# Filling three waits of TensorE with identity-times-ones matmuls in a two-block transformer kernel

## What is computed

```
first_block:  proj = rmsnorm(x) @ w_in ; two attentions (indexed sparse, latent)
              merged = sigmoid(g_a)*(o_a @ w_branch_a) + sigmoid(g_b)*(o_b @ w_branch_b)
              h = x + merged @ w_out
              h = h + (silu(gate)*val) @ w_down,   gate, val = conv(rmsnorm(h) @ w_up)
              x = rmsnorm(h)
second_block: h = [16 meta tokens; x] ; h = h + 0.5*swiglu(rms_norm(h))
              xn = rms_norm(h, norm_mix)
              merged = sum over 3 mixers of sigmoid(xn @ w_gate) * (y @ w_branch)
              h = h + merged @ w_out ; h = h + 0.5*swiglu(rms_norm(h))
              return rms_norm(h, final_norm)[:, 16:]
```

## Time and profile before

| | |
|---|---|
| median of 3 runs | 2298.59 us (2298.19 to 2300.34) |
| the profiled execution's own time | 2298.83 us |
| its span, first to last instruction | 2297.0 us |
| mean granted TensorE clock | 0.987 |
| TensorE matmul busy | 2209.4 us, 96% |
| DVE busy | 1257.7 us, 55% |
| ACT busy | 901.5 us, 39% |
| POOL busy | 220.3 us, 10% |

### The profile page before, as it was taken

The page is one execution under the profiler, slowest core; times in us unless marked ns, Lnnn a source line. Parts: engine busy times, 40 slices in busy tenths (PEclk is TensorE's granted clock), DMA queues, the critical chain, the costliest instruction groups (busy, mean ns, idle before and its releaser), DMA issues.

```text
span 2297.0 us, 35675 instructions
## 1 busy us (share of the span) xinstructions
PE 2209.4 (96%) x12408; PEld 1805.9 (79%) x12408; DVE 1257.7 (55%) x2672; ACT 901.5 (39%) x1803; POOL 220.3 (10%) x201
## 2 busy tenths in 40 slices
PE   6999999999999999999999799999999999999998
PEld 4557766777888889999999677777777777888887
DVE  5878877457745755542443545554545655443442
ACT  4465445444423444321232344443444433322333
POOL 0100033420000012000001000111100121000001
PEclk8999999999999999999999999999999999999999
DMA  3111211234443342333333222344333333333332
GB/s 104 38 38 39 65 42 51 60 106 139 145 135 88 94 151 76 89 117 101 91 90 101 73 80 80 79 102 105 94 84 100 84 92 92 91 104 89 91 108 74
DMA packets 400391, 205.64 MB, mean 90 GB/s; under 512 B 68956, under 2 KB 393928, under 8 KB 400284
## 3 DMA queue, kind: packets, MB, share of 16 engines
q1 hardware_dynamic: 399365, 203.83, 31.1%
q10 hardware_dynamic: 919, 0.43, 0.1%
HBM read 201.94 MB, written 14.80 MB: 94 GB/s over the span
## 4 chain that ended last, share of the span: by engine, by line
PE 82%; DVE 4%; ACT 2%; issue 2%; POOL 0%; DVEq 0%; ACTq 0%; POOLq 0%
PE acc L1159 52%; PE acc L1445 15%; PE acc L1205 5%; PE sco L1480 2%; PE acc L1544 1%; PE sco L1247 1%; PE acc L1540 1%; DVE w_lo L2219 1%; PE acc L1294 1%; PE sco L1520 1%; PE acc L1520 0%; PE sco L1500 0%; PE acc L1281 0%; PE sco L1271 0%; PE acc L1271 0%
## 5 line engine op out<-in xcount | busy, mean ns | idle before, releaser
L1672 ACT ACTIVATE w_hi<-raw 128x512 fp32r<-128x512 f32 (+4 forms) x656 | 371.9, 614 | 697.6 <-PE acc L1159 663.7
L2219 DVE TENSOR_TENSOR w_lo<-raw,w_hi 128x512 fp32r<-128x512 f32 (+4 forms) x656 | 425.1, 688 | 142.6 <-ACT w_hi L1672 138.3
L1159 PE MATMUL acc<-xn_hi,w_hi 128*128 128x512 f32 (+1 forms) x1408 | 421.0, 340 | 2.1 <-DVE qbuf L2769 2.1
L1159 PE MATMUL acc<-xn_lo,w_hi 128*128 128x512 f32 (+1 forms) x1408 | 422.0, 340 | 0.0
L1159 PE MATMUL acc<-xn_hi,w_lo 128*128 128x512 f32 (+1 forms) x1408 | 420.3, 339 | 0.0
L1159 PEld LDWEIGHTS acc<-xn_hi,w_hi 128*128 128x128 f32 x1408 | 241.9, 188 | 35.8 <-DVE qbuf L2769 3.0
L1159 PE MATMUL acc<-hid_hi,w_hi 128*128 128x512 f32 (+1 forms) x832 | 261.4, 349 | 7.0 <-DVE hid_lo L2711 7.0
L1159 PEld LDWEIGHTS acc<-xn_lo,w_hi 128*128 128x128 f32 x1408 | 241.2, 188 | 31.1 <-issue 0.5
L1159 PEld LDWEIGHTS acc<-xn_hi,w_lo 128*128 128x128 f32 x1408 | 241.5, 188 | 30.0
L1159 PE MATMUL acc<-hid_lo,w_hi 128*128 128x512 f32 (+1 forms) x832 | 263.0, 351 | 0.0
L1159 PE MATMUL acc<-hid_hi,w_lo 128*128 128x512 f32 (+1 forms) x832 | 262.2, 349 | 0.0
(11 more groups left out here) (393 smaller groups left out, 3040.7 us busy)
## 6 DMA issues: line engine op xcount, KB each, us to landing
raw<-in_w_ffn_in SPq DMA_DIRECT2D x176, 256.0 KB, 3.0
raw<-in_w_in SPq DMA_DIRECT2D x118, 256.0 KB, 3.1
raw<-in_w_up SPq DMA_DIRECT2D x88, 256.0 KB, 3.0
raw<-in_w_ffn_out SPq DMA_DIRECT2D x32, 384.0 KB, 3.4
raw<-in_w_gate SPq DMA_DIRECT2D x48, 256.0 KB, 3.2
raw<-in_w_ffn_out SPq DMA_DIRECT2D x32, 320.0 KB, 3.8
raw<-in_w_out SPq DMA_DIRECT2D x32, 256.0 KB, 3.1
bias<-grids_dram SPq DMA_DIRECT2D x64, 128.0 KB, 3.0
```

The source lines that it names most:

```text
L1159: mm = pe.matmul(acc[0:m, 2 * slot + b, 0:size], w[slot][:, t, 0:m], x[:, place(t), c:c + size], start=(t == 0 and w is w_hi and x is xh), ...
L1672: act.activation(w_hi[slot][:, a:b, :], raw[slot][:, a:b, :], ACT.Copy).then_inc(S[f"hi_ready{slot}"], parts)
L2219: dve.tensor_tensor(w_lo[slot][:, a:b, :], raw[slot][:, a:b, :], w_hi[slot][:, a:b, :].bitcast(F32), ALU.subtract).then_inc(S[f"split{slot ...
```

## The change

A helper `bridge(count)` issues `count` matmuls of 128 columns: `ones` stationary, `eye` moving, into the first 128 columns of bank 0 of `sco`. Nothing reads the result, no semaphore is waited for or raised. TensorE now issues 28 of them in each `resplit` phase, 28 in the norm phase ahead of the wait for `sq_added`, and 56 after the norm's sums. In all 140 matmuls are added, and nothing is removed.

```diff
+            def bridge(count):
+
+                for _ in range(count):
+                    pe.matmul(sco[:, 0, 0:P], ones[:, :], eye, start=True, stop=True)
+
...
+                elif kind == "resplit":
+                    bridge(28)
                 elif kind == "norm":
+                    bridge(28)
                     pe.wait_ge(S["sq_added"], n.at("sq_added", 0))
                     for b, (c, size) in enumerate(segs(ph[2])):
                         mm = pe.matmul(sco[:, 2 + b, 0:size], ones[:, :], square_sum[:, c:c + size], start=True,
                                        stop=True)
                     mm.then_inc(S["sq_used"], 1)
+                    bridge(56)
```

## The result

| | before | changed |
|---|---|---|
| median | 2298.96 us (2295.93 to 2300.34, 20 runs) | 2301.93 us (2299.41 to 2305.59, 20 runs) |
| span of the profiled execution | 2297.0 us | 2298.8 us |
| mean granted clock | 0.987 | 0.993 |

The medians differ by 3.0 us. The ratio is 1.0015, with a 95% interval from 1.0008 to 1.0021, which is +1.8 to +4.8 us; it is near the quotient of the means (2301.92 and 2298.55, +3.4 us), not of the medians. The forecast was 2303.5 in a range from 2300.5 to 2306.5. A second comparison with runs of their own gave 1.0017 (1.0008 to 1.0027), +3.5 us by medians and +4.2 by means. The change is slower, and most likely by less than the 0.2% that I had drawn as a line.

The account below looks back on a forecast made before the run. TensorE's stream, busy 96% of the span, was taken to bound the kernel. First resplit +0.9, norm +3.8 and second resplit -0.05 sum to +4.65 us on 2298.83, giving 2303.5 us, range 2300.5 to 2306.5.

Parts of the forecast that it names:

- Price of one added matmul: Each added matmul is two records and costs 0.223 us at 2.4 GHz; 28 take 6.25 us, 56 take 12.5.
- First resplit: `proj_out` starts 2.55 us later, the kept clock gives back 1.63 us; net +0.9 us.
- Second resplit: The bridge ends 2.58 us past the old start, offset by the full clock; net 0 to -0.1 us.
- Second norm: Both bridges in the norm outlast their waits and delay the first `mixers` item; net +3.8 us.
- the late sums: In the norm, 28 matmuls make the sums, root, reciprocal and all low parts 2.8 us late.
- the second bridge: 56 matmuls behind the norm's sums, 1279.3 to 1291.8, bring TensorE 5.7 us after the first low part.
- Clock: The granted clock would be 1.00 in both resplits and the norm, where it had fallen to half.
- The sum: Both resplits and the norm: +0.9 + 3.8 - 0.05 = +4.65 us.
- the cold clock costs next to nothing in this place: In the second norm DVE is late, and TensorE nearly keeps pace even at 1.2 GHz.
- The bridge that hides in its wait: Rival: at 0.112 us per added matmul each bridge ends before its wait does; 2294.6 us, chance 0.05.
- An absorption in `mixers`: Rival: later waits in `mixers` absorb part of the norm's 3.8 us, say half; 2301.6 us, chance 0.12.
- the second rival: The bridge doesn't keep the clock, TensorE stays at 1.2 GHz where it fell before; some 2330 us, chance 0.03.

Follow-up runs that it names:

- bridges in the norm alone: Against the kernel with 14 matmuls per resplit and 14 and 28 in the norm, resplit matmuls removed: 2298.75 us, ratio 1.0002.
- the bridges that fit: Changed kernel with half the added matmuls, 14 in each resplit, 14 and 28 in the norm: 2293.32 us (0.9979), repeated 2293.68 us (0.9982).
- the transposes: Changed kernel with each added matmul replaced by a transpose of the ones, same counts 28, 28, 56 and 28: 2293.32 us, ratio 0.9977.
- the seven-matmul bridges: Against the kernel with 28 added matmuls in each resplit and none in the norm, 7 in each resplit: 2295.93 us, ratio 0.9988.

## Why the prediction held

**Price of one added matmul.** Right, and the step that carries all the others. 56 records took 6.41 us with the last one 0.275, so their spacing is 6.14/55 = 0.112 us, that of the row with the same shape and type. The trace has 280 records of 140 matmuls. The bridges ended 2.5 us past the old start of `proj_out`, as summed: its first matmul stands 6.40 us behind the last branch matmul at both places, for 3.93 and 3.89 before.

**First resplit.** Expected +0.9, measured +0.88 us. **Second resplit.** Expected 0 to -0.1, measured -0.05.

**Second norm.** Expected +3.8, measured +3.77. Its parts held as well: the late sums, expected at +2.8, are +2.72 alone (24.47 less 21.75), and the second bridge adds 1.05 to them (25.52 less 24.47), where +1.0 was expected.

**Clock.** Right at the three places: 1.00 in every stretch behind a bridge. Over all thirteen profiled executions the clock fell to 0.50 at each of the ten resplits without a bridge, within the wait or up to 1.3 us behind it, and at none of the sixteen with one, be it of 7, 14 or 28.

**The sum.** The three places gave +4.60 us in the profiled executions, against +4.65. All executions together gave less: +3.0 and +3.5 us by medians, +3.4 and +4.2 by means. I read what the clock cost from one execution, and it varies.

In the norm, "the cold clock costs next to nothing in this place" holds for the first tiles of `mixers`, and does not for the norm's sums. In my execution the clock fell right behind them. In the kernels without a bridge in the norm it fell ahead of them twice (22.64, 22.66) and behind them three times (21.75), and the change saves these 0.9 us where they occur: 0.36 us on average over these five. This term is missing in my sum.

In the resplits, five executions without a bridge took 17.43, 17.40, 17.71, 16.84 and 16.84 us in the two stretches together, where the changed kernel takes 18.26. But in three of them the clock was still at 0.50 when the first stretch ended. This is the kernel with bridges in the norm alone, whose eleventh matmul started at 472.65:

```profile
467.60:472.60 5.00, 4.35 (x10) 3.47 (x11) 4.72 (x8) 2.51 (x5) 0.00 (x0) 0.50 0.36 108
472.70:474.20 1.50, 1.50 (x5) 1.21 (x4) 0.00 (x0) 0.00 (x0) 0.00 (x0) 0.50 0.00 0
474.40:476.00 1.60, 1.60 (x9) 1.28 (x8) 0.00 (x0) 0.00 (x0) 0.00 (x0) 1.00 0.00 0
```

What the clock still cost there stands in the part between resplit 1 and the norm: 800.90, 800.99 and 801.20 us in these three, for 800.44 in the kernel before, with the same spacing of 122.10 ns. With 0.46, 0.55 and 0.76 us added, the five are 17.43, 17.40, 18.17, 17.39 and 17.60, in the mean 17.6. So the change costs +0.66 us on average in the resplits, not the +0.83 of the profiled pair. That one execution lay this near the mean was luck.

Together this is 3.77 - 0.36 + 0.66 = +4.1 us, an estimate from these rows. It lies within both intervals, and so does the forecast. The same reckoning gives 17.6 - 13.3 + 0.36 = 4.7 us of gain for the bridges that fit, whose means lie 4.9 and 4.5 us under the kernel before; for the other kernels it agrees with the means to about 1 us. A difference of less than that I can't tell from chance.

**The rivals.** The bridge that hides in its wait didn't happen, and the transposes show that its mechanism is real at half the price. The clock was kept. An absorption in `mixers` didn't happen: from the norm to the second resplit the two kernels took 571.11 and 571.21 us. In the second rival I put the norm's two bridges about 20 us late; at its own price of 0.45 us for a matmul it is nearer 24, and nothing rests on it.

**Chances.** I gave 0.56 to a ratio above the line at 0.2% and 0.41 to one within it. It came out within, at 1.0015, and the line lies inside the interval.

## What to carry to other kernels

Filling a wait of TensorE to hold its clock pays as long as the filler overruns the wait by less than the kept clock gives back, which was 1.6 and 2.6 us in the two resplits. Size it by records in the trace, not by lines of the program: a plain fp32 matmul was two here, a transpose one. Take the price from a row of the same shape and type, sum it against the wait, and leave some room, since an empty remainder of 0.4 us cost nothing and 2.5 us of overrun ate the whole gain. Fill waits after which TensorE is the late engine. In the norm, where the next steps are those of other engines, 28 matmuls ahead of the sums cost 2.7 us, and bridges that fit gained nothing that could be measured (ratio 1.0002).

## What the runs showed that I had not expected

**Two paces of the same matmuls.** In the second block's first feed-forward some 3,000 matmuls of 264 columns run with no wait, and their mean spacing was 122.10 ns in eight profiled executions, 121.51 in four (the changed kernel, one of the two with bridges that fit, the transposes, the seven-matmul bridges) and 121.74 in one. That is up to 1.77 us of the span (371.23 against 373.00 for the same matmuls), with the clock at 1.00 in all. The same kernel had either. No run here shows what sets it.

**How much the clock wanders.** The last branch matmul ahead of the first resplit, before any edit here, started between 459.74 and 464.32 us in the profiled executions, as the granted clock fell for shorter or longer in setup and `front`. In eight of them the clock also fell once in `mixers`, at 1312 to 1325 us, and the part from the norm to the second resplit then took 572.5 to 573.3 us, not 571.1. So a single profiled execution cannot price an edit of 2 us by its span; the stretches between the same matmuls can.
